# Attention of the diff and moba stages placed between column blocks and output chunks

## The chip, the cores and the metric

The kernel runs on one core of one Trainium2 chip. The metric is the device time of one execution, in microseconds (us). The kernel before took 2924.59 us, the median of 3 runs (2924.18 to 2925.93). All arithmetic is in float32; the large matrix products are made of three products each, of a rounded "high" part and the remaining "low" part of both operands.

## The reference, cut to what matters

The model has 256 tokens of width 1024. Four layers of a first block, each ffn, mixer, ffn, are followed by two layers of a second block. The mixers of the first block are diff, moba, nsa, diff. Those that the change touches:

```
def diff_attention(h, w_in, w_out, lam, subln_g, lambda_init, pos):      # 8 heads
    q, k, v = split(h @ w_in, 3)                    # 1024 x 3072
    q, k = partial_rope(q), partial_rope(k)         # 16 rows of 64: two per head
    lam_full = exp(sum(lam[0] * lam[1])) - exp(sum(lam[2] * lam[3])) + lambda_init
    p = softmax over keys of (q . k) / 8, causal, for both rows c of a head
    a = p[:, :, 0] - lam_full * p[:, :, 1]
    o = a @ v                                       # v: 128 wide per head
    o = rms_norm(o, subln_g, 1e-5) * (1 - lambda_init)
    return o @ w_out

def moba_attention(h, w_in, w_out, pos):                                 # 16 heads
    q, k, v = split(h @ w_in, 3); q, k = partial_rope(q), partial_rope(k)
    # 256 tokens are one block: what is left is causal softmax attention, 64 wide
    return softmax(q . k / 8, causal) @ v @ w_out
```

## The kernel before

**Engines.** Each engine runs its own list of instructions in the order in which the program writes it; semaphores (`s_...`) are the only bond. SyncE (SP) loads the weights, 1 MB a tile, into four buffers RAW in the order of `plan`. Each tile holds two "splits". ScalarE (ACT) writes the high part of a split into HI (L1146 or, where a gain of the norm is folded in, two instructions on L1153), VectorE (DVE) the rest into LO (L1484, L1489). There are six HI and six LO buffers: split n can be made when TensorE (PE) has used split n-6 (`s_used`). `split(upto)` on either engine makes all splits before number `upto` that aren't made yet. `taken(n)` on PE waits for LO of split n.

**A mixer stage** (`st.w0` is its first split). PE projects six column blocks of 512 columns, four splits each: `first_block`, then `later_block` (L676), per split 2 row tiles x 6 matmuls of 128x512. In `first_block` the second row tile waits for its part of XL, which DVE makes in `second_rows` (L1636, `low`, L1525) from the transposes of H. ACT copies a finished block out of PSUM into TM (`copy_out`, L1279). DVE rotates q and k (`rotate`, L1690 to L1694). PE transposes each rotated block (`turns_of_qk`, L833, through `turned_block`), eight 128x128 transposes into PSUM banks 4 and 5, and ACT copies them to QT and KT (`turned_out`, L1288). The blocks come in the order q, q, k, k, v, v, and the attention begins when all six are there.

**The attention** goes by eight pairs i: `scores` (L772, banks 0/1 or 2/3 by turns, with a mask added by four bf16 matmuls), `maxima` on DVE (L1696), `exps` on ACT (L1295, four exponentials with sums), for diff the combination of the two rows on DVE (L1757 to L1768), `probs_turned` on PE (banks 4, 5), `probs` on ACT (L1307), `outputs` on PE (L807, banks 6 and 7 by turns), for diff `sums` of squares on ACT (L1342), roots on POOL (`outputs_roots`, L2071), and `in_place` on DVE (L1745, L1785), which writes M. PE runs scores two pairs ahead and issues eight matmuls of `clock` (L794) that nobody reads. For diff, the factor lambda is made on DVE and ACT after the sixth block (L1732 to L1743) from SGN and LM, which POOL loads at the start of the stage (L2083, L2084) after its loads of the next gains.

**The output projection.** `outputs_flipped` transposes four blocks of M a row tile (first half at pair 7), ACT and DVE make XH and XL of them (`high`, `low`), and `rows_by` (L688) runs eight chunks k of 128 rows of the weights, in two groups of four; each group runs row tile t = 0 over its chunks, then t = 1, six matmuls of 128x512 a chunk, accumulated in banks 4 to 7. The second half is flipped in the hook of chunk (k, t) = (3, 0); (4, 0) is the first to need it. `last_hook` transposes rows for the next stage.

**Steps of the loop on ACT and DVE before.** Both make splits one block ahead: after block n they make all before `w0 + 4n + 9` and then copy or rotate, as in

```
                for n in range(6):
                    if n >= 1:
                        split(st.w0 + 4 * n + 9)
                    copy_out(st, n, TM[:, :, n * 512:(n + 1) * 512], 2 * ((n + 1) % 2), 512)
```

## Time and profile before

| | |
|---|---|
| median of 3 runs | 2924.59 us |
| profiled execution, its own time | 2921.73 us |
| its span | 2919.9 us |
| PE busy | 2847.3 us, 98% |
| weight loads of PE | 2305.9 us, 79% |
| DVE busy | 1857.9 us, 64% |
| ACT busy | 1546.3 us, 53% |
| mean granted clock of PE | 0.996 |

The profile is of one execution. Busy time of an engine is the union of its instructions; matmuls overlap their neighbours, so a short idle stretch of PE can hide in the tail of the last one. The diff stages lie at 205 to 330 and 1782 to 1907 us of the span, moba at 714 to 838 us.

### The profile page before, as it was taken

What the parts mean: (1) busy time and instruction counts of PE and PEld (TensorE: products, weight loads), DVE (VectorE), ACT (ScalarE), POOL (GpSimd) and SP (SyncE); (2) the same over time, 40 slices, a digit from 0 to 9 for tenths busy, and PEclk for the clock granted to TensorE, in tenths of its full rate; (3) what the DMA queues carried; (4) which work ended last, traced back from release to release, by engine and by line L of the source; (5) the groups of instructions that cost most, each with busy time, mean ns of one, the idle gap of its engine ahead of it and who ended that gap; (6) DMA issues with size and microseconds to landing.
All of it is one profiled execution on the core that took longest, in us unless ns stands there. A gap on an engine that the chain in (4) does not pass through costs nothing.

```text
span 2919.9 us, 34940 instructions
## 1 busy us (share of the span) xinstructions
PE 2847.3 (98%) x13484; PEld 2305.9 (79%) x13484; DVE 1857.9 (64%) x2728; ACT 1546.3 (53%) x2656; POOL 149.1 (5%) x254
## 2 busy tenths in 40 slices
PE   8999999999999999999999999899999999999998
PEld 7877787887788788778887878788787788787786
DVE  6766776676567667646676776667654754645654
ACT  6546654654665365446654646665354444444442
POOL 1010100001000000100001000000100000000000
PEclk9999999999999999999999999999999999999999
DMA  8664467566446666551666675366664565654652
GB/s 261 217 222 162 142 213 242 182 225 215 159 152 216 231 191 229 201 162 44 195 222 218 216 250 184 100 216 227 213 229 145 186 202 186 215 193 137 188 187 87
DMA packets 358631, 559.42 MB, mean 192 GB/s; under 512 B 14625, under 2 KB 246049, under 8 KB 358209
## 3 DMA queue, kind: packets, MB, share of 16 engines
q1 hardware_dynamic: 350720, 535.02, 55.7%
q0 software_dynamic: 7600, 21.81, 2.2%
q8 instruction: 107, 1.75, 0.2%
q14 instruction: 60, 0.48, 0.1%
q10 hardware_dynamic: 144, 0.36, 0.0%
HBM read 556.03 MB, written 1.10 MB: 191 GB/s over the span
## 4 chain that ended last, share of the span: by engine, by line
PE 92%; DVE 5%; ACT 1%; issue 1%; POOL 1%; DMA 0%; SPq 0%; DVEq 0%; ACTq 0%; POOLq 0%
PE ps L640 38%; PE ps L701 26%; PE ps L646 19%; PE ps L610 4%; PE ps L813 1%; PE ps L782 1%; PE ps L760 1%; DVE LO L1484 1%; PE ps L928 0%; POOL ST L2021 0%; DVE XL L1525 0%; ACT SB L1303 0%; PE ps L790 0%; DVE M L1563 0%; DVE M L1602 0%
## 5 line engine op out<-in xcount | busy, mean ns | idle before, releaser
L640 PE MATMUL ps<-HI,XH 128*128 128x512 f32 (+1 forms) x2496 | 982.4, 394 | 5.6 <-DVE LO L1489 2.8
L640 PE MATMUL ps<-LO,XH 128*128 128x512 f32 (+1 forms) x2496 | 969.6, 389 | 0.0
L1484 DVE TENSOR_TENSOR LO<-RAW,HI 128x1024 fp32r<-128x1024 f32 x468 | 567.4, 1222 | 368.2 <-ACT HI L1146 366.7
L646 PE MATMUL ps<-HI,XL 128*128 128x512 f32 (+1 forms) x2496 | 769.5, 389 | 0.3
L1146 ACT ACTIVATE HI<-RAW 128x1024 fp32r<-128x1024 f32 x468 | 490.2, 1058 | 488.7 <-PE ps L701 320.2
L1489 DVE SCALAR_TENSOR_TENSOR LO<-RAW,GC,HI 128x512 fp32r<-128x512 f32 (+1 forms) x896 | 622.2, 744 | 188.9 <-ACT HI L1153 186.3
L1153 ACT ACTIVATE HI<-RAW,GC 128x512 fp32r<-128x512 f32 (+1 forms) x896 | 587.9, 714 | 157.8 <-PE ps L646 130.7
L640 PEld LDWEIGHTS ps<-HI,XH 128*128 128x128 f32 x2496 | 469.3, 188 | 102.0 <-DVE LO L1489 4.4
L646 PEld LDWEIGHTS ps<-HI,XL 128*128 128x128 f32 x2496 | 466.6, 188 | 103.4 <-DVE XL L1525 6.8
L640 PEld LDWEIGHTS ps<-LO,XH 128*128 128x128 f32 x2496 | 469.8, 188 | 91.8
L701 PE MATMUL ps<-HI,AH 128*128 128x512 f32 x880 | 281.3, 401 | 0.0
L701 PE MATMUL ps<-LO,AH 128*128 128x512 f32 x880 | 277.6, 397 | 0.0
L701 PE MATMUL ps<-HI,AL 128*128 128x512 f32 x880 | 277.4, 396 | 0.0
L701 PEld LDWEIGHTS ps<-HI,AH 128*128 128x128 f32 x880 | 162.6, 188 | 57.1 <-issue 20.7
L701 PEld LDWEIGHTS ps<-HI,AL 128*128 128x128 f32 x880 | 165.8, 188 | 40.5
L701 PEld LDWEIGHTS ps<-LO,AH 128*128 128x128 f32 x880 | 165.7, 188 | 40.3
L1247 ACT ACTIVATE AH<-ps 128x512 fp32r<-128x512 f32 x110 | 65.8, 598 | 191.2 <-PE ps L610 191.2
L1648 DVE TENSOR_TENSOR AL<-ps,AH 128x512 fp32r<-128x512 f32 x110 | 75.9, 690 | 107.7 <-ACT AH L1247 107.7
L1266 ACT ACTIVATE SG<-ps,ST 128x256 f32<-128x256 f32 x176 | 74.0, 471 | 132.7 <-PE ps L646 132.7
L1662 DVE SCALAR_TENSOR_TENSOR AF<-ps,ST,SG 128x256 f32<-128x256 f32 x176 | 77.0, 479 | 84.7 <-ACT SG L1266 84.7
L1519 DVE SCALAR_TENSOR_TENSOR ACC<-RAW,CS,ACC 128x512 f32<-128x512 f32 x168 | 126.2, 751 | 5.1
L701 PE MATMUL ps<-HI,XH 128*128 128x512 f32 x288 | 91.7, 400 | 10.8 <-DVE LO L1484 4.3
(182 smaller groups left out, 1990.0 us busy)
## 6 DMA issues: line engine op xcount, KB each, us to landing
RAW<-in_ffn_w_in SPq DMA_DIRECT2D x350, 512.0 KB, 4.9
RAW<-in_ffn_w_out SPq DMA_DIRECT2D x88, 1024.0 KB, 5.0
RAW<-in_w_ada SPq DMA_DIRECT2D x48, 1024.0 KB, 5.2
RAW<-in_w_in SPq DMA_DIRECT2D x44, 1024.0 KB, 5.2
RAW<-in_w_ffn_in SPq DMA_DIRECT2D x88, 512.0 KB, 4.8
RAW<-in_diff_w_in SPq DMA_DIRECT2D x24, 1024.0 KB, 5.1
RAW<-in_w_ffn_out SPq DMA_DIRECT2D x22, 1024.0 KB, 4.9
RAW<-in_moba_w_in SPq DMA_DIRECT2D x12, 1024.0 KB, 5.1
```

The source lines that it names most:

```text
L610: i = e.transpose(dst[:, c * P:(c + 1) * P], v, ident)
L640: e.matmul(ps[:, b + t, 0:nw], XH[:, k, t * P:(t + 1) * P], q[s][:, c * nw:(c + 1) * nw], start=(k == 0 and q is HI), stop=False)
L646: i = e.matmul(ps[:, b + t, 0:nw], XL[:, k, t * P:(t + 1) * P], HI[s][:, c * nw:(c + 1) * nw], start=False, stop=(k == 7))
L701: i = e.matmul(ps[:, 4 + 2 * t + nh, :], x(k, t), q[s][:, nh * 512:nh * 512 + 512], start=(k == 0 and q is HI and x is th), stop=(k == chu ...
L1146: e.activation(HI[n % NSPLIT][:, 0:t.width], RAW[t.buf][:, h * t.width:(h + 1) * t.width], ACT.Copy).then_inc(s_hi, 1)
L1153: i = e.activation(HI[n % NSPLIT][:, c * w:(c + 1) * w], RAW[t.buf][:, h * t.width + c * w:h * t.width + (c + 1) * w], ACT.Copy, scale=g[c])
L1266: o = e.activation(SG[:, i, t], ps[:, b + t, 0:S], ACT.Silu, scale=r)
L1484: e.tensor_tensor(LO[n % NSPLIT][:, 0:w], RAW[t.buf][:, at[1] * w:(at[1] + 1) * w], HI[n % NSPLIT][:, 0:w].bitcast(F32), ALU.subtract).the ...
L1489: i = e.scalar_tensor_tensor(out=LO[n % NSPLIT][:, c * w2:(c + 1) * w2], in0=RAW[t.buf][:, at[1] * w + c * w2:at[1] * w + (c + 1) * w2], s ...
L1519: e.scalar_tensor_tensor(out=A, in0=src, scalar=CS[:, kc:kc + 1], in1=A, op0=ALU.mult, op1=ALU.add).then_inc(s_ada, 1)
L1648: e.tensor_tensor(AL[:, 2 * jp:2 * jp + 2, :], ps[:, b, :].rearrange("p (j n) -> p j n", j=2), AH[:, 2 * jp:2 * jp + 2, :].bitcast(F32), A ...
L1662: o = e.scalar_tensor_tensor(out=AF[:, i, t], in0=ps[:, b + t, S:2 * S], scalar=root_of(st, t)[0], in1=SG[:, i, t], op0=ALU.mult, op1=ALU. ...
```

## The change

A stage's work is now placed by a counter `at`. On PE, `at = 4n + k2` is the place ahead of split k2 of block n (4 to 23), 24 the place between the last block and the output chunks, and 25 to 32 the places behind the chunks (k, t) = (0, 0) to (3, 0) and (0, 1) to (3, 1). ACT and DVE loop over the same `at` and write their part of each step there.

The columns are loaded by pairs of heads: blocks 0 and 1 hold q and k of pairs 0 to 3 (256 columns each), block 2 the v of these, and blocks 3 to 5 the same for pairs 4 to 7. A tile of q and k is two DMAs of 512 KB. `QK` takes the place of QT and KT; the rotation has its own room `R` instead of M. PSUM: scores in banks 6 and 7 (the last pair in 2 and 3), turned probabilities in 4 and 5 (the last two pairs in 0 and 1), outputs in bank 5 for pairs 0 to 3 and 0 to 3 for the others. The matmuls of `clock` in these stages are gone. POOL's part is unchanged.

```diff
+PAIR_BLOCKS = ((0, 1024), (256, 1280), (2048,), (512, 1536), (768, 1792), (2560,))
+QK_BLOCKS = (0, 1, 3, 4)
+QK_AT = (6, 10, 18, 22)
+SCORES_AT = (7, 9, 13, 16, 19, 21, 23, 25)
+TURNED_AT = (9, 11, 15, 18, 21, 23, 27, 29)
+OUTPUTS_AT = (13, 14, 16, 19, 25, 26, 28, 30)
+HALF_AT = 22
+SCORE_BANK = (6, 6, 6, 6, 6, 6, 6, 2)
+TURNED_BANK = (4, 4, 4, 4, 4, 4, 0, 0)
+OUTPUT_BANK = (5, 5, 5, 5, 0, 1, 2, 3)
...
@@ block.tensor
                 for k2 in range(4):
+                    if between is not None:
+                        between(4 * n + k2)
                     w = st.w0 + 4 * n + k2
                     taken(w)
...
+                def turned_qk(q):
+                    n = QK_BLOCKS[q]
+                    e.wait_ge(s_rt, c["rt"] + q + 1)
+                    if q == 1:
+                        e.wait_ge(s_pt, c["pt"] + 1)
...
+                def pair_scores(i):
+                    q = i // 2
+                    if i % 2 == 0:
+                        e.wait_ge(s_tn, c["tn"] + 2 * q + 2)
+                    if i == 7:
+                        e.wait_ge(s_ol, c["ol"] + 2)
+                    elif i >= 1:
+                        e.wait_ge(s_ex, c["ex"] + i)
...
+                def pair_turned(i):
+                    e.wait_ge(s_df if diff else s_ex, c["df" if diff else "ex"] + i + 1)
+                    if i < 6:
+                        e.wait_ge(s_tn, c["tn"] + 2 * sum(at <= TURNED_AT[i] for at in QK_AT))
+                        if 1 <= i:
+                            e.wait_ge(s_pt, c["pt"] + i)
+                        placed = sum(at < TURNED_AT[i] for at in OUTPUTS_AT)
+                        if placed:
+                            e.wait_ge(s_o, c["o"] + placed * out)
+                    elif i == 6:
+                        e.wait_ge(s_o, c["o"] + 6 * out)
+                    else:
+                        e.wait_ge(s_pt, c["pt"] + 7)
...
+                def pair_outputs(i):
+                    e.wait_ge(s_cp, c["cp"] + (3 if i < 4 else 6))
+                    e.wait_ge(s_pt, c["pt"] + sum(at < OUTPUTS_AT[i] for at in TURNED_AT))
+                    if 1 <= i < 4:
+                        e.wait_ge(s_o, c["o"] + i * out)
+                        if OUTPUTS_AT[i] > QK_AT[2]:
+                            e.wait_ge(s_tn, c["tn"] + 6)
+                    elif i >= 6:
+                        e.wait_ge(s_ex, c["ex"] + 8)
...
+                def attention(at):
+                    if at in QK_AT:
+                        turned_qk(QK_AT.index(at))
+                    if at in TURNED_AT:
+                        pair_turned(TURNED_AT.index(at))
+                    if at in OUTPUTS_AT:
+                        pair_outputs(OUTPUTS_AT.index(at))
+                    if at in SCORES_AT:
+                        pair_scores(SCORES_AT.index(at))
+                    if at == HALF_AT:
+                        e.wait_ge(s_cp, c["cp"] + 5)
+                        half_flipped(0, 2)
...
-                        later_block(st, n, 512)
+                        later_block(st, n, 512, attention)
...
+                e.wait_ge(s_pt, c["pt"] + 6)
+                e.wait_ge(s_ex, c["ex"] + 7)
+                attention(24)
...
+                def ready(k, t):
+                    if k == 0:
+                        e.wait_ge(s_ol, c["ol"] + t + 1)
+                    elif k == 4:
+                        e.wait_ge(s_ol, c["ol"] + t + 3)
+                def hook(k, t):
+                    if k < 4:
+                        attention(25 + k + 4 * t)
+                    if (k, t) == (3, 1):
+                        half_flipped(1, 0)
+                    last_hook(st, k, t, 8)
...
@@ block.scalar
+                for at in range(33):
+                    if at in (4, 8, 12, 16, 20, 24):
+                        block_out(at // 4 - 1)
+                    if at - 1 in SCORES_AT:
+                        i = SCORES_AT.index(at - 1)
+                        if i == 0 and diff:
+                            lambdas()
+                        exps(st, i, SCORE_BANK[i])
+                    if 4 <= at < 24:
+                        split(st.w0 + at + 6)
+                    if at in QK_AT:
+                        q = QK_AT.index(at)
+                        turned_out(st, q, QK[:, q])
+                    if at in TURNED_AT:
+                        i = TURNED_AT.index(at)
+                        probs(st, i, nj, TURNED_BANK[i])
+                    if at in OUTPUTS_AT and diff:
+                        sums(OUTPUTS_AT.index(at))
+                    if at == HALF_AT:
+                        for t in range(2):
+                            high(t, 0, 2 + t, s_of, c["of"] + t + 1, s_oh)
+                for t in range(2):
+                    high(t, 1, t, s_of, c["of"] + t + 3, s_oh)
+                split(st.w1 + 2)
...
@@ block.vector
+            def by_places(st, softened, placed, placed_after):
+                TM, QK = st.t["TM"], st.t["QK"]
+                second_rows(st)
+                for at in range(33):
+                    if 4 <= at < 24:
+                        split(st.w0 + at + 5)
+                    if at in SCORES_AT:
+                        i = SCORES_AT.index(at)
+                        maxima(st, i, SCORE_BANK[i])
+                    if at % 4 == 0 and at // 4 - 1 in QK_BLOCKS:
+                        n = at // 4 - 1
+                        rotate(st, QK_BLOCKS.index(n), TM[:, :, n * 512:(n + 1) * 512].rearrange("p t (h d) -> p t h d", d=64),
+                               8, cst("c8"), cst("s8"), n, st.t["R"])
+                    if at - placed_after in OUTPUTS_AT:
+                        placed(OUTPUTS_AT.index(at - placed_after))
+                    if at - 1 in SCORES_AT:
+                        softened(SCORES_AT.index(at - 1))
+                    if at == HALF_AT:
+                        for t in range(2):
+                            low(t, 0, 2 + t, s_oh, st.c["oh"] + t + 1, s_ol)
+                for t in range(2):
+                    low(t, 1, t, s_oh, st.c["oh"] + t + 3, s_ol)
+                split(st.w1 + 2)
...
@@ diff on block.vector
+                def lambdas():
+                    e.wait_ge(s_mixw, c["mixw"] + 32)
+                    e.tensor_scalar(SGN[:, :], SGN[:, :], 1.0 - linit, None, ALU.mult).then_inc(s_sgn, 1)
+                    e.tensor_tensor(LM[:, 0:4:2, :], LM[:, 0:4:2, :], LM[:, 1:4:2, :], ALU.mult).then_inc(s_lam, 1)
+                    e.wait_ge(s_lam, c["lam"] + 1)
+                    e.tensor_reduce(LS[:, 0:2], LM[:, 0:4:2, :], AX.X, ALU.add).then_inc(s_lam, 1)
...
+                def softened(i):
+                    if i == 0:
+                        lambda_full()
                     reciprocals(st, i)
...
+                phase(st)
+                lambdas()
+                by_places(st, softened, placed, 1)
...
@@ moba on block.vector
+                by_places(st, softened, placed, 0)
```

`placed` is `in_place` of before. `softened` is the reciprocals and, in diff, the combination.

## Rows read from the trace of the kernel before

**Rows 1.** The page, busy time and share of the span by engine.

```profile
PE 2847.3 (98%) x13484; PEld 2305.9 (79%) x13484; DVE 1857.9 (64%) x2728; ACT 1546.3 (53%) x2656; POOL 149.1 (5%) x254
```

**Rows 2.** Timeline of PE, a diff stage's blocks: start, duration, engine, line, operation, tiles.

```profile
240.22 0.48 PE L640 MATMUL ps<-HI,XH 128*128 128x512 f32 x1
...
251.22 1.03 PE L610 MATMUL ps<-CST,TM 128*128 128x128 f32 x8
```

**Rows 3.** Stretches: width, busy time (and instructions) of each engine, granted clock, DMA.

```profile
275.00:306.00 31.00, 23.63 (x184) 16.63 (x185) 23.70 (x80) 25.53 (x106) 6.00 (x14) 1.00 0.06 19
```

**Rows 4.** Timeline of PE, scores of two pairs in the diff attention.

```profile
287.42 0.93 PE L782 MATMUL ps<-KT,QT 64*128 64x128 f32 x8
...
289.68 0.93 PE L782 MATMUL ps<-KT,QT 64*128 64x128 f32 x8
```

**Rows 5.** Timeline of PE, start of moba's attention; in brackets idle before, and releaser.

```profile
785.56 0.93 PE L782 MATMUL ps<-KT,QT 64*128 64x128 f32 x8 [1.45 <-ACT TM L1279]
...
787.85 2.80 PE L796 MATMUL ps<-CST 128*128 128x384 f32 x8
```

**Rows 6.** Timeline of ACT behind the first column block of a diff stage.

```profile
216.96 1.27 ACT L1279 ACTIVATE TM<-ps,ST 128x512 f32<-128x512 f32 x2 [3.73 <-PE ps L646]
218.12 8.69 ACT L1153 ACTIVATE HI<-RAW,GC 128x512 fp32r<-128x512 f32 x14
```

**Rows 7.** Timeline of DVE: low parts; reciprocals and combination of a pair.

```profile
219.60 9.36 DVE L1489 SCALAR_TENSOR_TENSOR LO<-RAW,GC,HI 128x512 fp32r<-128x512 f32 x14
...
300.70 0.18 DVE L1707 RECIPROCAL RC<-SM 128x4 f32<-128x4 f32 x1
...
301.17 0.75 DVE L1766 SCALAR_TENSOR_TENSOR SB<-SB,CF 128x128 f32<-128x128 f32 x2
```

**Rows 8.** The chain that ended last: exponentials of two pairs.

```profile
278.95 3.33 ACT SB L1303 x16
```

**Rows 9.** Timeline of PE: the first use of XL's second row tile.

```profile
212.23 0.62 PE L646 MATMUL ps<-HI,XL 128*128 128x512 f32 x2
```

**Rows 10.** Timeline of POOL: issue of the load of LM.

```profile
215.91 0.54 POOL L2084 DMA_DIRECT2D LM<-in_diff_lambda  x1
```

**Rows 11.** The tile LM: from issue to landing.

```profile
DMA to landing us min/median/max: 4.6/5.3/6.0
```

**Rows 12.** Timeline of ACT: a table load and its activation, in nsa.

```profile
1287.92 1.28 ACT L1381 ACT_TABLE_LOAD   x1
1289.22 0.28 ACT L1381 ACTIVATE GS<-TM 128x96 f32<-128x96 f32 x1
```

**Rows 13.** Timeline of PE: last outputs of diff, flips of the second half.

```profile
305.36 0.91 PE L813 MATMUL ps<-TM,PT 128*128 128x128 f32 x6 [1.00 <-DVE M L1752]
...
311.58 1.03 PE L610 MATMUL ps<-CST,M 128*128 128x128 f32 x8
```

**Rows 14.** Timeline of DVE: the last placing, low parts of the second half.

```profile
308.39 0.61 DVE L1752 SCALAR_TENSOR_TENSOR M<-ps,ST,SGN 128x128 f32<-128x128 f32 x2
...
312.85 1.29 DVE L1525 TENSOR_TENSOR XL<-ps,XH 128x512 fp32r<-128x512 f32 x2 [2.71 <-ACT XH L1172]
```

**Rows 15.** The page, costliest groups: busy and mean ns, idle before them.

```profile
L1484 DVE TENSOR_TENSOR LO<-RAW,HI 128x1024 fp32r<-128x1024 f32 x468 | 567.4, 1222 | 368.2 <-ACT HI L1146 366.7
```

**Rows 16.** Timeline of PE: the three gaps over 2 us after the start.

```profile
1288.87 14.02 PE L928 MATMUL ps<-RAW,E 128*60 128x256 f32 x64 [2.08 <-DVE E L1827]
...
1372.87 0.73 PE L701 MATMUL ps<-HI,XH 128*128 128x512 f32 x2 [2.17 <-DVE LO L1484]
...
2100.85 1.97 PE L610 MATMUL ps<-CST,M 128*128 128x128 f32 x8 [2.04 <-DVE M L1614]
```

**Rows 17.** Stretches behind these gaps; the column before the last two is the granted clock.

```profile
1290.00:1300.00 10.00, 10.00 (x48) 6.19 (x47) 0.00 (x0) 1.18 (x2) 0.00 (x0) 1.00 0.60 196
...
1374.00:1377.00 3.00, 3.00 (x9) 2.32 (x8) 3.00 (x3) 0.61 (x1) 0.00 (x0) 0.50 0.59 157
...
2104.00:2108.00 4.00, 4.00 (x11) 3.13 (x10) 4.00 (x6) 2.18 (x5) 0.00 (x0) 0.54 0.40 103
```

More of the change, by code:

```diff
@@ L196, in tile_cols, with tiles_pairs, dst @@
                              2 * nw, what, st))
+        def tiles_pairs(w, st):
+            for cols in PAIR_BLOCKS:
+                for half in range(2):
+                    src = w[half * 512:(half + 1) * 512, :].rearrange("(c p) n -> p c n", p=P)
+                    n = 512 // len(cols)
+                    loads = []
+                    for g, c0 in enumerate(cols):
+                        def dst(r, g=g, n=n):
+                            return r[:, :].rearrange("p (c g n) -> p c g n", c=4, n=n)[:, :, g, :]
+                        loads.append((dst, src[:, :, c0:c0 + n]))
+                    plan.append(Tile("w", loads, HW, None, st))
         def tiles_proj(w, st):
@@ L226, in build @@
             else:
-                tiles_proj(a[f"{st.kind}_w_in"][st.j], st)
+                (tiles_proj if st.kind == "nsa" else tiles_pairs)(a[f"{st.kind}_w_in"][st.j], st)
                 if st.kind == "nsa":
@@ L886, in diff_or_moba @@
-            def diff_or_moba(st):
+                out = 2 if diff else 1
+                def turned_qk(q):
[3 more added lines that the diff above has]
+                        e.wait_ge(s_pt, c["pt"] + 1)
+                    elif q == 2:
+                        e.wait_ge(s_pt, c["pt"] + 3)
+                        e.wait_ge(s_o, c["o"] + 3 * out)
+                    elif q == 3:
+                        e.wait_ge(s_pt, c["pt"] + 5)
+                    for t in range(2):
+                        i = turn(ps[:, 4 + t, :], [TM[:, t, n * 512 + j * P:n * 512 + (j + 1) * P] for j in range(4)])
+                    i.then_inc(s_tb, 1)
@@ new lines, in pair_turned @@
+                def pair_turned(i):
[11 more added lines that the diff above has]
+                        e.wait_ge(s_pt, c["pt"] + 7)
+                    for j in range(nj):
+                        o = turn(ps[:, TURNED_BANK[i] + j, :], [SB[:, i % 3, j, m * P:(m + 1) * P] for m in range(3)])
+                    o.then_inc(s_pf, 1)
@@ new lines, in half_flipped @@
+                def half_flipped(half, b):
+                    e.wait_ge(s_o, c["o"] + 4 * (half + 1) * out)
+                    for t in range(2):
+                        flip(t, half, b + t, s_of)
+                def attention(at):
[10 more added lines that the diff above has]
+                        half_flipped(0, 2)
@@ L1327, in diff_or_moba, with block_out @@
                 second_rows(st)
-                for n in range(6):
-                    if n >= 1:
-                        split(st.w0 + 4 * n + 9)
+                def block_out(n):
                     copy_out(st, n, TM[:, :, n * 512:(n + 1) * 512], 2 * ((n + 1) % 2), 512)
-                    if 1 <= n <= 4:
-                        X = QT if n < 3 else KT
-                        turned_out(st, n - 1, X[:, 4 * ((n - 1) % 2):4 * ((n - 1) % 2) + 4, :])
-                for i in range(2):
-                    exps(st, i)
-                if diff:
-                    LS = st.t["LS"]
-                    e.wait_ge(s_lam, c["lam"] + 2)
-                    e.activation(LS[:, 2:4], LS[:, 0:2], ACT.Exp).then_inc(s_lex, 1)
                 def sums(i):
@@ L1674, in ffn, with rotate @@
                 split(st.w1 + 2)
-            def rotate(st, n, v, half, cos, sin):
+            def rotate(st, n, v, half, cos, sin, block=None, free=None):
                 nh = v.shape[2]
                 size = 2 * nh * half
-                R = [M[:, :, :].rearrange("p a b -> p (a b)")[:, j * size:(j + 1) * size]
-                     .rearrange("p (t h d) -> p t h d", t=2, h=nh) for j in range(4)]
+                free = M[:, :, :].rearrange("p a b -> p (a b)") if free is None else free
+                R = [free[:, j * size:(j + 1) * size].rearrange("p (t h d) -> p t h d", t=2, h=nh) for j in range(4)]
                 cb, sb_ = (f.rearrange("p (t d) -> p t d", t=2).unsqueeze(2).to_broadcast([P, 2, nh, half])
@@ L1725, in diff @@
             def diff(st):
                 c, x = st.c, st.t
[L1727 removed]
+                SB, SM, RC, CF, LM, LS, SGN = (x[v] for v in ("SB", "SM", "RC", "CF", "LM", "LS", "SGN"))
                 linit = 0.8 - 0.6 * math.exp(-0.3 * st.i)
[L1729 to L1732 removed]
```

176 lines of the change are left out of this document (58 added, 118 removed).

## Prediction

> **What bounds the kernel now.** I read the page first: TensorE is busy 98% of the span [rows 1], so time moves only by PE work that goes or by PE waits that come or go. The clock is full nearly everywhere. Then the stretches by engine and the timeline of PE: within a diff stage PE runs without a hole through the six column blocks, about 2.75 us for each quarter block of 12 matmuls (11.0 us between the turns of two blocks [rows 2]), until the attention starts. That takes 31.0 us [rows 3], and 0.2 before it in which PE could have gone on. A pair of heads costs PE 2.26 us from one scores to the next where nothing holds it [rows 4], eight pairs 18.1 us, the eight turns of outputs about 0.8: 18.9 us of need. The other 12.3 us are waits and the eight matmuls of `clock`. In moba, whose pairs have twice the turns and outputs, PE is full but for 1.45 us of wait plus 0.2 of pipeline tail, and 2.7 of `clock` [rows 5]: 4.3 us. So all that the change can win is 2 x 12.3 + 4.3 = 28.9 us, 1.0% of the run.
>
> **What it takes away.** Exactly that: `clock` goes, and the chain scores, maxima, exponentials, combination, turn, outputs of each pair is stretched over slots that hold other matmuls. I credit the whole 28.9 us. The PE work itself is the same in number; but each group put between projections costs the first matmul behind it 0.08 to 0.1 us (0.48 instead of 0.39 in [rows 2]), some 15 new places a stage: 1.2 us x 3 = 3.6 us.
>
> **What it adds: waits.** Queues are in order, so I follow each engine's written order through a stage, with slot n meaning `at == n`, and time 0 at the place named. The costs: copy of a block out of PSUM, done 1.4 us after the last matmul; a high part 1.24 (8.69 for seven) [rows 6]; a low part 1.34 (9.36 for seven) [rows 7]; turned copies 1.1, a little under the two copies of the same size in [rows 6]; exponentials of a pair 1.65 (3.33 for two) [rows 8]; reciprocal to combined probabilities 1.2 (300.70 to 301.92 [rows 7]); rotation 1.35 (from the copy's end to the first low part in [rows 6, 7]).
>
> 1. Head of each diff stage. VectorE now runs `lambdas` before `second_rows`, and `lambdas` waits for the two loads of POOL's software queue. The second is issued at 215.91 and lands 4.6 to 6.0 us later, median 5.3 [rows 10, 11]: 221.2. POOL's issue is untouched: it follows the row roots. Three small operations (0.8) and the first low part of XH (0.65) bring 222.7. PE wants that low part for the second row tile at 212.23 [rows 9]. Wait: 10.5 us (9.8 to 11.2 by the landing). Before, this DVE work sat behind the sixth block, and nobody waited for the loads.
> 2. Slot 6, all stages. VectorE now makes three low parts before it rotates block 0. First high part ready at 2.6 after slot 4 starts; low parts until 6.65; rotation until 8.1. Slot 6 starts at 5.5: 2.7 us (before, the rotation came first).
> 3. Slot 9. The exponentials of pair 0 stand behind `block_out(1)` on ScalarE. From the start of slot 8: copy to 1.4, table load and its follower 1.3 (1287.92 to 1289.22 [rows 12]), in diff the small exponential 0.25, exponentials to 4.65, combination to 5.9. PE is at slot 9 after 2.75: 3.15 us in diff; moba waits for the exponentials alone: 1.7.
> 4. Slot 14, diff: one bank (5) for outputs 0 to 3, and the placing of outputs 0 stands behind maxima and a low part: 0.7.
> 5. Slot 18: the transposes of block 3 and the turned probabilities share bank 4, so PE waits for a high part (1.24 + 0.2) and the turned copies (1.1), less the 0.8 of its own turns: 1.8 in all three.
> 6. Slot 21: as 3, behind `block_out(4)`, and on VectorE behind a rotation and a placing: ready at 4.95 against 2.75, 2.2 in diff; 0.35 in moba.
> 7. Before the output rows: PE waits for the exponentials of pair 6, which stand behind `block_out(5)`: 1.4 + 1.65 + 0.1 = 3.15 in all three. This is the old start of the attention, kept, without the maxima.
> 8. Slot 27, diff: turned pair 6 waits for outputs 5 to be placed. From outputs to placed takes 3.6 us (305.36 to 309.0 [rows 13, 14]), and the squares now stand behind the exponentials of pair 7: ready about 9.1 after the rows start, PE there at 6.8: 2.3.
> 9. The second half of the rows: the flip comes directly before the chunk that needs it. From the flip's start the two low parts end after 2.56 (311.58 to 314.14 [rows 13, 14]); behind them VectorE still has to make the weights' low part of that very chunk (`split(st.w0 + at + 5)` ends one short), 1.22 [rows 15]. 3.85 less 0.8 of flips: 3.05 in all three, and 0.3 more in diff for the last placing. Before, the flip had a whole group of chunks ahead of its use.
>
> Sum of diff: 10.5 + 2.7 + 3.15 + 0.7 + 1.8 + 2.2 + 3.15 + 2.3 + 3.35 = 29.85. Sum of moba: 2.7 + 1.7 + 1.8 + 0.35 + 3.15 + 3.05 = 12.75. Two diff stages and moba: 72.45 us of waits, + 3.6 of switches, - 28.9: **+47 us**. Each of the places could be off by 0.5 us; places that are hidden after all would have to give 47 us back.
>
> **The clock.** Waits have a second price. In this trace three gaps of PE passed 2 us in mid-run: after 2.17 us the granted clock was soon 0.50, for 3 us at least; after 2.04 eight transposes took 1.97 us, where they take 1.03 at full clock [rows 2], and the 4 us behind them had 0.54; after 2.08 it stayed at 1.00 [rows 16, 17]. The levels are 1.2 and 2.4 GHz. The first cost at least 1.5 us, the second 0.9 + 1.8. The change makes some 7 gaps over 2 us in a diff stage and 3 in moba, 17 in all; two of three, at 2.1, is 24 us, of which some 4 fall where PE would wait anyway: I take **+20**, between 0 (none falls) and 40 (all fall).
>
> **Other parts.** A block's tile is loaded in two DMAs with 1 KB rows instead of one with 2 KB. The ffn stages load so already, and SP's waits do not change: 0, up to 1 us a stage. The table load is not new, only earlier: one in each stage. The page "ScalarE: Activation LUTs" of the Trainium skill, section What ACT_TABLE_LOAD costs, says that a switch of tables costs 2.66 us with a drain behind the load. The trace does not agree: the load of 1.28 us is followed by its activation 1.30 us after its start [rows 12]. By the page, place 3 would be 1.4 longer in each stage, 4 us in all; I go by the row.
>
> **The number.** The profiled execution took 2921.7 us (span 2919.9). 2921.7 + 47 + 20 = 2988.7; the median of the runs shown is 2.9 higher: 2992.
>
> **Rivals.**
> - The waits as worked out, but the clock holds through gaps of 3 us, as it held through one of 2.08: 2972. For it: the attention of before ran with gaps up to 1.45 us at 1.00. Against it: two of three. 0.15.
> - The waits, and every gap over 2 us lowers the clock, for as long as after 2.04: 3012 to 3020. 0.10.
> - The loads of `lambdas` land early or the head wait costs much less, since PE's first matmuls of the second tile and the clock hide part: two times 10.5 go, with it 4 of clock: 2967. The issue time is in the trace, so 0.06.
> - It does what it says and is faster: VectorE and ScalarE, busy 23.7 and 25.5 of the 31 us [rows 3], get slack from the projections around them, so each chain fits into its two slots. The place is the PE queue, the price 28.9 less 3.6: 2899. It decides the sign once the waits of a diff stage stay under 11 us and of moba under 3. Places 1 and 9 alone are 13.8 in diff, and neither depends on how loaded an engine is, only on the written order. 0.03.
> - Only two fifths of the waits come, 29 us: + 3.6 - 28.9 is +4, 2928, no change that can be told: 0.03.
> - Forecast, 2992, within 15 us: the rest, 0.63.
>
> What a measurement of this kernel can tell from no change is about 0.2%, 5.8 us. Slower by more than that 0.94, within it 0.03, faster 0.03. The range runs from 2957 (the waits 10 us shorter and no clock lost, or no head wait) to 3014 (nearly all gaps at the lower clock).
>
> **What would show it.** In the waits of PE of the changed kernel: a wait of about 10 us on a low part of XH near 212 us and once more near 1800; one near 3 us on the transposes of TM, released by DVE's rotation, three times; waits of about 3 us on the exponentials before the first output chunk and on a low part of weights at the fifth chunk, three times each; no matmul of `clock` but at the start and in nsa. The stretch from the first column matmul of a diff stage to its last output matmul should grow by 17 to 28 us, of moba by 9 to 14. A granted clock under 1.00 should show behind the long gaps. I am wrong if PE passes from the sixth block into the output rows without a hole, or if the first low part of the second row tile is made before the two loads land; a time under 2925 would mean that the engines do not keep the written order as I read it.

## The result

The changed kernel took 2990.9 us (median of 4 runs, 2988.5 to 2991.5) beside 2924.5 for the kernel before in the same comparison (4 runs, 2924.2 to 2925.9). The ratio is 1.0225, 95% interval 1.0207 to 1.0242: 66.4 us slower. 2992 had been forecast.

The page of the changed kernel, busy time by engine (the row that answers to [rows 1]; its span is 2989.0 us, the mean granted clock 0.985 where it was 0.996):

```profile
PE 2867.2 (96%) x13460; PEld 2316.9 (78%) x13460; DVE 1855.3 (62%) x2728; ACT 1543.8 (52%) x2656; POOL 150.1 (5%) x254
```

PE did 24 matmuls fewer (those of `clock`, 8.4 us by [rows 5] three times) and was still busy 19.9 us longer: the matmuls that stayed took 28 us more, the switches between groups included. The other engines did what they had done.

Where PE waited, by the line that waits and the instruction waited for: total, times, longest. Only the lines that are new or have grown:

```profile
PE ps L679 <- DVE XL L1628: 17.1, 2, 8.6
PE ps L736 <- DVE LO L1587: 12.4, 8, 2.7
PE ps L643 <- DVE SB L1886: 10.1, 4, 3.1
...
PE ps L736 <- issue: 9.0, 3, 3.0
PE ps L643 <- DVE TM L1797: 7.7, 3, 2.6
PE ps L643 <- DVE M L1897: 5.6, 4, 2.4
...
PE ps L643 <- issue: 4.9, 4, 1.6
...
PE ps L643 <- ACT SB L1397: 1.9, 2, 1.7
...
PE ps L848 <- DVE M L1897: 1.2, 2, 0.6
```

Names of the changed kernel: L679 and L673 are the column blocks, L736 the output rows, L643 transposes, L817 scores, L848 outputs; on DVE L1628 is `low`, L1797 the end of the rotation, L1886 the combination, L1897 the placing, L1587 and L1592 low parts of weights. Counts of 3 are one in each changed stage, of 2 one in each diff stage. Of the eight waits on L1587, five (4.3 us) stand in the kernel before too; the other three are 8.1.

The same waits in order of time, in the first diff stage. This is the timeline of PE, its rows with idle time before them:

```profile
221.14 1.22 PE L679 MATMUL ps<-HI,XL 128*128 128x512 f32 x2 [8.62 <-DVE XL L1628]
...
235.81 1.97 PE L643 MATMUL ps<-CST,TM 128*128 128x128 f32 x8 [2.57 <-DVE TM L1797]
...
250.87 0.55 PE L643 MATMUL ps<-CST,SB 128*128 128x128 f32 x3 [3.11 <-DVE SB L1886]
...
271.76 0.91 PE L848 MATMUL ps<-TM,PT 128*128 128x128 f32 x6 [0.62 <-DVE M L1897]
...
275.88 0.52 PE L643 MATMUL ps<-CST,SB 128*128 128x128 f32 x3 [0.48 <-DVE M L1897]
...
288.99 0.52 PE L643 MATMUL ps<-CST,SB 128*128 128x128 f32 x3 [1.56 <-issue]
...
301.59 0.55 PE L643 MATMUL ps<-CST,SB 128*128 128x128 f32 x3 [1.94 <-DVE SB L1886]
...
318.00 1.19 PE L736 MATMUL ps<-HI,XH 128*128 128x512 f32 x2 [3.01 <-issue]
...
330.10 0.52 PE L643 MATMUL ps<-CST,SB 128*128 128x128 f32 x3 [2.35 <-DVE M L1897]
...
344.63 1.22 PE L736 MATMUL ps<-HI,XH 128*128 128x512 f32 x2 [2.71 <-DVE LO L1587]
```

Read the durations too. Two matmuls of 128x512 in a row took 0.62 us before [rows 9], and 1.22 here at 221.14. Eight transposes of TM took 1.03 [rows 2], and 1.97 here at 235.81. Those ran at half clock. The stretches say the same (width, busy time of PE, PEld, DVE, ACT and POOL, granted clock, DMA share, GB/s; the first beside [rows 9] and [rows 10], where PE had no hole):

```profile
205.00:225.00 20.00, 11.38 (x46) 8.83 (x45) 8.74 (x17) 7.64 (x20) 5.41 (x9) 0.75 0.31 96
...
248.00:262.00 14.00, 11.13 (x56) 8.91 (x57) 7.74 (x19) 9.55 (x28) 0.00 (x0) 0.88 0.31 87
262.00:275.00 13.00, 12.38 (x67) 9.92 (x66) 8.46 (x19) 8.73 (x26) 2.12 (x4) 1.00 0.43 150
...
318.00:330.00 12.00, 9.75 (x42) 7.43 (x42) 4.85 (x17) 3.22 (x16) 1.81 (x4) 0.75 0.01 1
```

From the first matmul of the diff stage to the first of the next stage it was 124.9 us before (204.76 to 329.69) and is 153.2 (204.89 to 358.08): 28.3 longer. In moba 123.9 (713.92 to 837.81) became 138.3 (742.30 to 880.60): 14.4 longer. The second diff stage went from 124.9 (1782.42 to 1907.34) to 150.9 (1825.18 to 1976.04), 25.9 longer. The three are 68.6 us, of the 69.1 by which the span grew.

How much of this is clock can be added up: PE's busy time in stretches of 1 us, times what the granted clock lacks of 1.00. Over the three stages that gives 25.2 us here (11.4, 4.8 and 9.0), and 0.0 in the kernel before. Below it is called the clock sum.

### The profile page after: what moved, and what is told of

Read it like the earlier page. It is cut to its first block, busy times and chain, and to the rows that moved or that the text cites. A ratio compares the mean times of both kernels' runs of the same rounds, so it can differ in the third digit from the quotient of the medians.

```text
span 2989.0 us, 34946 instructions
## 1 busy us (share of the span) xinstructions
PE 2867.2 (96%) x13460; PEld 2316.9 (78%) x13460; DVE 1855.3 (62%) x2728; ACT 1543.8 (52%) x2656; POOL 150.1 (5%) x254
## 4 chain that ended last, share of the span: by engine, by line
PE 89%; DVE 6%; ACT 2%; issue 2%; POOL 1%; DMA 1%; SPq 0%; DVEq 0%; ACTq 0%; POOLq 0%
PE ps L673 36%; PE ps L736 26%; PE ps L679 18%; PE ps L643 4%; PE ps L848 2%; PE ps L817 1%; DVE LO L1592 1%; PE ps L795 1%; DVE LO L1587 1%; DVE XL L1628 1%; POOL ST L2136 1%; ACT JUNK L1259 0%; PE ps L1021 0%; PE ps L825 0%; ACT TM L1372 0%
## 5 line engine op out<-in xcount | busy, mean ns | idle before, releaser
L673 PE MATMUL ps<-HI,XH 128*128 128x512 f32 (+1 forms) x2496 | 989.5, 397 | 5.6 <-DVE LO L1592 2.3
L673 PE MATMUL ps<-LO,XH 128*128 128x512 f32 (+1 forms) x2496 | 972.9, 390 | 0.0
L679 PE MATMUL ps<-HI,XL 128*128 128x512 f32 (+1 forms) x2496 | 772.8, 391 | 17.3 <-DVE XL L1628 17.1
L1587 DVE TENSOR_TENSOR LO<-RAW,HI 128x1024 fp32r<-128x1024 f32 x468 | 566.3, 1222 | 341.9 <-ACT HI L1239 340.6
L1592 DVE SCALAR_TENSOR_TENSOR LO<-RAW,GC,HI 128x512 fp32r<-128x512 f32 (+1 forms) x896 | 622.3, 744 | 205.3 <-ACT HI L1246 204.2
L679 PEld LDWEIGHTS ps<-HI,XL 128*128 128x128 f32 x2496 | 468.4, 189 | 122.4 <-DVE XL L1628 24.7
L673 PEld LDWEIGHTS ps<-HI,XH 128*128 128x128 f32 x2496 | 471.9, 189 | 102.5 <-DVE LO L1592 4.3
L673 PEld LDWEIGHTS ps<-LO,XH 128*128 128x128 f32 x2496 | 472.2, 189 | 91.6
L736 PE MATMUL ps<-HI,AH 128*128 128x512 f32 x880 | 281.3, 401 | 0.0
L736 PE MATMUL ps<-LO,AH 128*128 128x512 f32 x880 | 277.6, 397 | 0.0
L736 PE MATMUL ps<-HI,AL 128*128 128x512 f32 x880 | 277.4, 396 | 0.0
L736 PEld LDWEIGHTS ps<-HI,AH 128*128 128x128 f32 x880 | 162.6, 188 | 57.1 <-issue 20.7
L736 PEld LDWEIGHTS ps<-HI,AL 128*128 128x128 f32 x880 | 165.8, 188 | 40.5
L736 PEld LDWEIGHTS ps<-LO,AH 128*128 128x128 f32 x880 | 165.7, 188 | 40.3
L736 PE MATMUL ps<-HI,XH 128*128 128x512 f32 x288 | 97.4, 420 | 27.8 <-DVE LO L1587 12.4
```

What stands on the lines that cost most here:

```text
L673: e.matmul(ps[:, b + t, 0:nw], XH[:, k, t * P:(t + 1) * P], q[s][:, c * nw:(c + 1) * nw], start=(k == 0 and q is HI), stop=False)
L679: i = e.matmul(ps[:, b + t, 0:nw], XL[:, k, t * P:(t + 1) * P], HI[s][:, c * nw:(c + 1) * nw], start=False, stop=(k == 7))
L736: i = e.matmul(ps[:, 4 + 2 * t + nh, :], x(k, t), q[s][:, nh * 512:nh * 512 + 512], start=(k == 0 and q is HI and x is th), stop=(k == chu ...
L1587: e.tensor_tensor(LO[n % NSPLIT][:, 0:w], RAW[t.buf][:, at[1] * w:(at[1] + 1) * w], HI[n % NSPLIT][:, 0:w].bitcast(F32), ALU.subtract).the ...
L1592: i = e.scalar_tensor_tensor(out=LO[n % NSPLIT][:, c * w2:(c + 1) * w2], in0=RAW[t.buf][:, at[1] * w + c * w2:at[1] * w + (c + 1) * w2], s ...
```

## The experiments

The theory under test: the loss is a handful of waits that come from the order in which DVE and ACT are written, plus the clock that the gaps cost. If so, orders alone must undo it, with the places, banks and loads left as they are. The rivals: the waits are only where PE happens to stand, so that one removed comes back at the next place; or the waits matter and the clock does not.

**`lambdas` later.** The changed kernel, with DVE's part of `lambdas` moved from ahead of `second_rows` to place 6:

```diff
-                lambdas()
-                by_places(st, softened, placed, 1)
+                by_places(st, softened, placed, 1, lambdas)
@@ in by_places, behind the split of each place
+                    if at == 6 and early is not None:
+                        early()
```

> The changed kernel with one step moved back: in a diff stage VectorE does the operations on SGN and LM at place 6, behind the low parts of the second row tile, and no longer ahead of them. My theory (the order written on each engine makes the waits): the two waits of PE on XL, 8.6 and 8.4 us, go, and with them the stretch at the lower clock behind them, some 2 us each: 22 us less than the 2991 of the changed kernel, about 2969. Rival 1 (only the wait counts, not the clock): 17 less, 2974. Rival 2 (the loads of SGN and LM are late for whoever wants them, so the wait only moves to place 6 or 9): nothing regained, 2985 to 2991.

Measured: 2973.1 us (2970.3 to 2974.9), ratio 1.0162 [1.0147, 1.0177], 17.8 us under the changed kernel. Both waits on XL of 8.6 us are gone, and 205 to 225 us is at clock 1.00. But 17.8 is hardly more than the two waits, 17.1: the time is rival 1's. It is not that the clock costs nothing: the clock sum is 25.6 us, where it was 25.2. What the head no longer costs is lost elsewhere. Stretches of 4 us show one such place. First the changed kernel behind its head gap (first row) and behind the gap at slot 9, then this kernel behind its gap at slot 9:

```profile
221.00:225.00 4.00, 3.86 (x9) 3.12 (x10) 2.00 (x4) 0.00 (x0) 0.00 (x0) 0.50 0.16 37
...
250.00:254.00 4.00, 3.13 (x19) 2.35 (x20) 3.33 (x9) 2.28 (x5) 0.00 (x0) 0.80 0.20 24
254.00:258.00 4.00, 4.00 (x20) 3.30 (x19) 2.42 (x6) 2.67 (x10) 0.00 (x0) 0.78 0.63 239
```

```profile
239.00:243.00 4.00, 2.89 (x16) 1.91 (x16) 2.31 (x6) 2.54 (x5) 0.00 (x0) 0.59 0.11 13
243.00:247.00 4.00, 4.00 (x13) 3.14 (x12) 3.24 (x9) 1.72 (x8) 0.00 (x0) 0.55 0.67 249
```

The same gap of 3.11 us cost more clock here (0.59 and 0.55) than there (0.80 and 0.78). The head gap cost 8.6 us of wait and 2.3 of slower matmuls: from slot 6's transposes back to the stage's start the stretch is 10.96 us shorter (235.81 less 224.85). From these transposes to the outputs at slot 14 it is 37.5 us here (224.85 to 262.34) and was 35.95 (235.81 to 271.76): 1.5 of the 2.3 came back. Whether this is because the head gap no longer stands ahead of it isn't shown. The gap of 2.6 at slot 6 stands 12 us ahead of it in both kernels, and in the second diff stage of the changed kernel, behind a head gap of 8.4 and the same gap at slot 6, the gap of 3.11 left the clock at 1.00:

```profile
1871.78 0.55 PE L643 MATMUL ps<-CST,SB 128*128 128x128 f32 x3 [3.11 <-DVE SB L1886]
```

```profile
1872.00:1876.00 4.00, 4.00 (x27) 3.04 (x26) 3.46 (x7) 2.38 (x10) 0.00 (x0) 1.00 0.44 110
```

So one gap at one place has no fixed price in clock; a number can be given for the sum only.

**The gaps filled.** The changed kernel, with matmuls that nobody reads in front of the long waits:

```diff
@@ tokens_by, ahead of the matmuls with XL
+                if beside is not None:
+                    beside()
@@ first_block
+                              (lambda: clock(12)) if st.kind == "diff" and k2 == 0 else None).then_inc(s_used, 1)
@@ turned_qk
+                    if q == 0:
+                        clock(3)
                     e.wait_ge(s_rt, c["rt"] + q + 1)
@@ pair_turned
+                    if i == 0:
+                        clock(4 if diff else 2, 5)
                     e.wait_ge(s_df if diff else s_ex, c["df" if diff else "ex"] + i + 1)
@@ ahead of the output rows
                 e.wait_ge(s_pt, c["pt"] + 6)
+                clock(4, 4)
                 e.wait_ge(s_ex, c["ex"] + 7)
@@ hook of the chunk (3, 1)
                         half_flipped(1, 0)
+                        clock(3, 2)
```

> The changed kernel with matmuls that nobody reads put ahead of five waits of PE, each group a little shorter than the gap that it fills: 24 at the head of a diff stage (8.2 of 8.6 us), 6 at place 6, 8 at place 9 (4 in moba), 8 ahead of the output rows, 6 ahead of chunk (4, 0). The waits end when they did; only the idleness goes. My theory (a gap lowers the granted clock and that is a price of its own, forecast at 20 us): the clock stays near 1.00 in these stages and the time falls by 15 to 25, to about 2971. Rival (the clock falls but PE would have waited anyway, or the lower clock costs nothing here): 2988 to 2993, and if the groups are too long, more.

Measured: 2974.4 us (2973.5 to 2975.3), ratio 1.0167 [1.0152, 1.0182]: 16.6 us less, with all the waits' causes in place. The mean clock rose from 0.985 to 0.993, and the first stretch (PE's 19.07 us include the filling) to 1.00:

```profile
205.00:225.00 20.00, 19.07 (x78) 13.45 (x77) 8.58 (x17) 7.57 (x20) 5.41 (x9) 1.00 0.33 100
```

The clock sum fell from 25.2 to 3.4. So the clock cost at least 16.6 us; the filling doesn't reach every gap and can itself delay work.

**Exponentials first.** The changed kernel, with ACT's copy of a block behind the exponentials at slots 8, 20 and 24:

```diff
-                    if at in (4, 8, 12, 16, 20, 24):
+                    if at in (4, 12, 16):
                         block_out(at // 4 - 1)
...
                         exps(st, i, SCORE_BANK[i])
+                    if at in (8, 20, 24):
+                        block_out(at // 4 - 1)
```

> The changed kernel with one order changed on ScalarE: at places 8, 20 and 24 the exponentials come ahead of the copy of the finished block. My theory: the wait before the output rows (3.0 us in three stages) goes whole; at place 9 moba's 1.7 goes and diff keeps about 1.5 of 3.1, since VectorE still rotates block 1, which needs the copy, ahead of the combination; place 21 stays in diff for the same reason. Waits regained: 3 x 3.0 + 2 x 1.6 + 2.0 = 14, with the clock behind the gap at the rows some 5 more: about 2972. Rival (the copy comes later by as much, and the rotation, the turns and outputs 4 wait for it): 2985 to 2991.

Measured: 2974.6 us (2973.9 to 2977.4), ratio 1.0170 [1.0154, 1.0185], 16.4 less. The three waits of 3.0 before the output rows fell to 1.1 in all, moba's on the exponentials are gone, and that on the combination at slot 9 is 2.1 instead of 3.1, with the table load still in the chain; 11.7 of the 16.4 are these waits:

```profile
PE ps L643 <- DVE SB L1888: 8.2, 4, 2.1
...
PE ps L736 <- issue: 1.1, 3, 0.4
```

**The head alone, in the kernel before.** The kernel before, with DVE's operations on SGN and LM ahead of `second_rows`, and nothing else:

```diff
-                second_rows(st)
-                for n in range(6):
-                    projected(st, n, TM, n * 512, 512 if n < 4 else 0)
+                phase(st)
                 e.wait_ge(s_mixw, c["mixw"] + 32)
                 e.tensor_scalar(SGN[:, :], SGN[:, :], 1.0 - linit, None, ALU.mult).then_inc(s_sgn, 1)
-                for i in range(2):
-                    maxima(st, i)
                 e.tensor_tensor(LM[:, 0:4:2, :], LM[:, 0:4:2, :], LM[:, 1:4:2, :], ALU.mult).then_inc(s_lam, 1)
...
                 e.tensor_reduce(LS[:, 0:2], LM[:, 0:4:2, :], AX.X, ALU.add).then_inc(s_lam, 1)
+                second_rows(st)
+                for n in range(6):
+                    projected(st, n, TM, n * 512, 512 if n < 4 else 0)
+                for i in range(2):
+                    maxima(st, i)
```

> The kernel before with one part of the change alone: VectorE does the operations on SGN and LM at the head of a diff stage, ahead of the low parts of the second row tile. My theory: PE waits about 8.5 us in each of the two diff stages and runs some us at the lower clock behind it: +21, 2945. Rival 1 (no price of the clock): +17, 2941. Rival 2 (the wait comes from something else that the change brings, as the loads in halves): 2924 to 2928.

Measured: 2948.1 us (2946.5 to 2950.6), ratio 1.0079 [1.0062, 1.0096]: 22.9 us for two waits of 8.7, so 5.6 beyond them. The clock sum is 7.9, of it 4.8 behind the head; the rest lies in the attention, where PE also waits. The order of three small operations accounts for a third of what the change lost, without any of the change's own work.

```profile
PE ps L646 <- DVE XL L1525: 17.3, 2, 8.7
```

**Rotation and low part.** The changed kernel, with block 0 rotated ahead of the low part of place 4, and the low part that the chunk (4, 0) needs made at place 24:

```diff
-                    if 4 <= at < 24:
+                    if 4 < at < 24:
                         split(st.w0 + at + 5)
...
+                    if at == 24:
+                        split(st.w0 + 29)
```

> The changed kernel with two orders changed on VectorE: at place 4 it rotates block 0 ahead of the three low parts, and at place 24 it also makes the low part of the fifth chunk's weights. My theory: the wait at place 6 (2.6 us) goes in three stages, the one ahead of chunk (4, 0) shrinks by 1.2, together 11.4, and some 4 us of lower clock behind them: about 2976. Rival 1 (no price of the clock): 2979.5. Rival 2 (the low parts are then late for PE at places 5 to 7): 2985 to 2991.

Measured: 2978.4 us (2968.2 to 2981.2), ratio 1.0175 [1.0160, 1.0190], 12.5 less. Slot 6 no longer waits (7.7 us gone), and the wait on the late low part went down by 7.4; but `low` of XL now ends last before (4, 0), 1.1 each time, 3.3 more in all: of 3.05 forecast for that place a third is the flip itself. The waits account for 11.8 of the 12.5, so hardly any clock came back; at 2978.4 the time lies nearer to rival 1 (2979.5) than to 2976.

```profile
PE ps L736 <- DVE XL L1628: 7.3, 7, 1.1
...
PE ps L736 <- DVE LO L1587: 5.0, 8, 2.2
```

**All orders together.** The three order changes above, ACT's copy of the turned block ahead of the high part at slot 18, and DVE's combination ahead of its rotation and placing:

```diff
+                    if at == 18:
+                        turned_out(st, 2, QK[:, 2])
                     if 4 <= at < 24:
                         split(st.w0 + at + 6)
...
                         maxima(st, i, SCORE_BANK[i])
+                    if at - 1 in SCORES_AT:
+                        softened(SCORES_AT.index(at - 1))
                     if at % 4 == 0 and at // 4 - 1 in QK_BLOCKS:
...
                         placed(OUTPUTS_AT.index(at - placed_after))
-                    if at - 1 in SCORES_AT:
-                        softened(SCORES_AT.index(at - 1))
```

> The changed kernel with all these orders changed at once: operations on SGN and LM at place 6, rotation of block 0 first, exponentials ahead of the block copy at 8, 20 and 24, the combination ahead of rotation and placing, turned copies of block 3 ahead of the high part, low part of the fifth chunk's weights at place 24. Waits that should go, from the changed kernel's trace: diff 8.5 + 2.6 + 3.1 + 1.9 + 3.0 + 1.2 + 1.2 = 21.5, twice; moba 2.6 + 1.7 + 0.1 + 3.0 + 1.2 + 1.2 = 9.8; 53 in all, and most of the lower clock, 17: about 2921, between 2915 and 2932. So my theory says that the placing itself is sound and about even with the kernel before, and that the written order cost all the rest. Rival (new waits take the place of these, engines being behind): 2940 or more.

Measured: 2928.8 us (11 runs, 2927.6 to 2933.2), ratio 1.0016 [1.0007, 1.0025]. Orders alone gave back 62 of the 66 us; the 2921 expected was missed by 8. Slot 18 gave back 0.35 of its 1.2. What was left had in part been made by the last edit: with the combination ahead, the placing came late, and the one bank of outputs 0 to 3 held PE at slot 14 for 2.3 us instead of 0.6, and slot 27 as before for 2.4:

```profile
PE ps L643 <- DVE M L1905: 7.9, 8, 2.4
...
PE ps L848 <- DVE M L1905: 4.6, 2, 2.3
```

**The kernel before without `clock`.** One line less, the eight matmuls of each diff and moba stage:

```diff
                     scores(st, i, row(QT, i), row(KT, i))
-                clock()
```

> The kernel before without the eight matmuls of clock in the diff and moba stages. My theory: they lie where PE would wait for exponentials anyway, so at most 0.7 us a stage comes back, 2923 to 2925, if the clock holds; if it falls in the gap of 2 us or more that they leave, some 2 us a stage more: up to 2932. Rival (they cost their whole 2.7 us in each of three stages): 2916.

Measured: 2928.8 us (10 runs, 2924.3 to 2931.4), ratio 1.0012 [1.0003, 1.0021]. That is 3.7 us more than the 2925.1 beside it. The matmuls are worth what they take and a little more: their 2.7 us a stage became waits for exponentials and combination, and behind these the clock fell:

```profile
280.84 0.97 PE L782 MATMUL ps<-KT,QT 64*128 64x128 f32 x8 [1.88 <-ACT SB L1302]
...
284.14 0.90 PE L610 MATMUL ps<-CST,SB 128*128 128x128 f32 x3 [1.79 <-DVE SB L1765]
```

```profile
280.00:290.00 10.00, 7.37 (x50) 5.30 (x51) 6.44 (x24) 6.56 (x30) 0.00 (x0) 0.66 0.00 1
```

**The loads in two DMAs.** The kernel before, with each tile of the diff and moba columns as two DMAs of 512 KB with 1 KB rows:

```diff
+                for half in range(2):
...
+                    for g in range(2):
+                        loads.append((dst, src[:, :, c0 + 256 * g:c0 + 256 * g + 256]))
```

> The kernel before with one part of the change alone: each tile of the diff and moba column blocks in two DMAs of 512 KB with rows of 1 KB, columns in the old order. My theory: nothing waits for these loads, 2923 to 2926. Rival (the loads in halves are late or slow): 2928 or more.

Measured: 2924.2 us (10 runs, 2921.5 to 2925.6), ratio 0.9996 [0.9987, 1.0005]: no cost that can be told.

**The orders mended.** From the waits that were left in the kernel with all orders: the combination goes ahead of placing and rotation only at slots 8 and 20, the turned block's copy goes ahead of the high part at slot 6 too, and the turned pair 6 goes to bank 2, where it needs no placing. ACT and DVE also make the split of the sixth chunk's weights (`split(st.w0 + 30)`) at places 30 and 31 instead of at the end. The parts that aren't orders of ACT or DVE, and DVE's places 8 and 20:

```diff
-TURNED_BANK = (4, 4, 4, 4, 4, 4, 0, 0)
+TURNED_BANK = (4, 4, 4, 4, 4, 4, 2, 0)
...
                     elif i == 6:
-                        e.wait_ge(s_o, c["o"] + 6 * out)
+                        e.wait_ge(s_ex, c["ex"] + 8)
                     else:
                         e.wait_ge(s_pt, c["pt"] + 7)
+                        e.wait_ge(s_o, c["o"] + 6 * out)
...
+                    if at in (8, 20):
+                        softened(SCORES_AT.index(at - 1))
+                        if at - placed_after in OUTPUTS_AT:
+                            placed(OUTPUTS_AT.index(at - placed_after))
```

> The pairs version with all order changes of e6_all_orders, and what its remaining waits point to: the combination goes ahead of the placing and rotation only at slots 8 and 20; the copies of the turned pair stand before the high part at slots 6 and 18; the turned pair 6 goes to another bank. In e6_all_orders each diff stage still held TensorE at slots 7 (0.61 us), 14 (2.31), 21 (1.02) and 27 (2.40) on VectorE's placing. Theory (what is left of the loss is these in-order waits): each diff stage loses 1.7 less at slot 14, 2.4 less at slot 27, 0.9 less at slot 21 and 0.6 less at slot 7, 5.6 us in all, each moba stage 0.9, so 2928.7 - 13 = 2915.7, and a few us of clock with it: 2912 to 2917, faster than before. Rival (VectorE is nearly full in these stretches, so that a wait removed at one slot comes back at the next): at or above 2925, with new waits of TensorE on VectorE's low parts or flips of the same sum.

Measured: 2910.9 us (5 runs, 2908.2 to 2912.9) beside 2925.8, ratio 0.9950 [0.9936, 0.9963]: 14.9 us faster than the kernel before, and 80 faster than the change as it was made. Its busy time, and all waits of PE in the first diff stage (205 to 330 us):

```profile
PE 2841.4 (98%) x13460; PEld 2300.6 (79%) x13460; DVE 1855.5 (64%) x2728; ACT 1543.2 (53%) x2656; POOL 150.1 (5%) x254
```

```profile
PE ps L643 <- issue: 1.2, 1, 1.2
PE ps L736 <- DVE XL L1634: 1.1, 1, 1.1
PE ps L848 <- DVE M L1913: 0.6, 1, 0.6
PE ps L643 <- DVE M L1913: 0.5, 1, 0.5
PE ps L736 <- issue: 0.4, 1, 0.4
```

3.8 us where the changed kernel has 27, with the same work on every engine and the same places. So waits taken away did not come back elsewhere. The clock sum is 0.0 again.

## Why the prediction was right, step by step

**The sign** was right, and by the reason given: all nine places are in the trace. Seven have the named releaser; the trace puts slot 18 and the wait before the output rows down to PE's own issue. The second fell from 3.0 to 0.4 with ACT's exponentials ahead of its copy, so the experiment names it. At slot 18 PE goes on at 288.99, 0.1 us after ACT's two copies of the turned block end (287.83 to 288.89 on its timeline). With these copies ahead of the high part the wait fell only from 1.6 to 1.2: most of it is the copies themselves, which can't start before PE's own transposes end. The place was right; what it owed to the high part is 0.35.

**The sizes of the waits**, forecast and found in us: head 10.5, 8.6; slot 6 2.7, 2.6; slot 9 3.15, 3.1 (moba 1.7, 1.7); slot 14 0.7, 0.6; slot 18 1.8, 1.6; slot 21 2.2, 1.9 (moba 0.35, 0.25); before the rows 3.15, 3.0; slot 27 2.3, 2.35; chunk (4, 0) 3.35 in diff and 3.05 in moba, 2.7 in both. One of 0.5, at the second placing, was not forecast. A diff stage has 27.0 instead of 29.85, moba 11.8 instead of 12.75: 65.5 in all where the sum had 72.45. For slot 18 and chunk (4, 0) the sum took PE's own eight turns as 0.8 us, though [rows 13] have 1.03; slot 18's turns took 1.03 and chunk (4, 0)'s 1.09, and both waits came out shorter for it. The switches were priced against a matmul of 0.39, which stands in none of the rows shown; PE's timeline before has one at 204.76 us.

Most of what is missing is the head. Its term took the landing of LM from the kernel before, 5.3 us after the issue [rows 11]. In the changed kernel it landed in 3.5:

```profile
DMA to landing us min/median/max: 3.4/3.5/3.6
```

So the size of the head wait did not follow from the written order alone, as the prediction had it. The wait seems to shorten its own cause: while PE stands, SP's weight loads stop, and the DMA engines are busy 0.31 of 205 to 225 us instead of 0.50. In the five kernels whose head waits the median is 3.4 to 3.6, and 4.8 to 5.3 in the six whose head doesn't. With the gaps filled, where PE is busy (19.07 of 20 us) and the DMA share stays at 0.33, it is 3.5 as well, so it isn't the idle PE that matters; that the emptier DMA engines do is what is left, and was not tested by itself.

**The place of the table load** was right, and with it the row's price instead of the page's. In the timeline of ACT at slot 8:

```profile
245.08 1.27 ACT L1372 ACTIVATE TM<-ps,ST 128x512 f32<-128x512 f32 x2 [2.60 <-PE ps L679]
246.36 1.28 ACT L1438 ACT_TABLE_LOAD   x1
247.66 0.20 ACT L1438 ACTIVATE LS<-LS 128x2 f32<-128x2 f32 x1
```

The load follows the copy by 0.01 us and is followed by its activation after 1.30. The page "ScalarE: Activation LUTs" of the Trainium skill, section What ACT_TABLE_LOAD costs, adds a drain of 1.38 us to a load of 1.28. This trace agrees with the load and shows no drain behind it; with one, as an estimate by that page, slot 9 would have waited 4.5 us and not 3.1.

**What was credited and the switches.** The mended kernel tests both: its waits are 3.8 + 3.8 + 2.7 = 10.3 us, so 10.3 + 3.6 of switches - 28.9 gives -15.0 against the kernel before, and -14.9 was measured. The two terms were right together, to the 4 us of the interval; nothing here tests them one by one. That `clock` taken out alone costs 3.7 us is no contradiction: what it covered is now covered by projections.

**The clock** was the term with the wrong size. 66.4 - 65.5 - 3.6 + 28.9 leaves 26 us for it, where 20 was taken, within the bounds of 0 to 40. The clock sum, read from the trace by itself, is 25.2, and the filling gave 16.6 back. (Between the two profiled executions the three stages grew by 68.6, which would leave 28; some 3 us of that are not placed.) The working was 17 gaps, two of three falling, 2.1 us each, less 4 us that would be hidden. In the changed kernel 13 of the 17 (1.94 us and longer) had a granted clock under 1.00 in the 4 us behind them; the four others are slot 6 in moba, slot 21 in the first diff stage, and slots 9 and 27 in the second. 25.2 over 13 is 1.9 each, as an average. So the price of a gap was about right, more of them fell, and the 4 us off have nothing in the trace to stand on. The form was rough as well: the model had a gap over 2 us as the condition, but without `clock` the granted clock fell behind gaps of 1.8 and 1.9 us, and it held behind one of 3.11. That the total came out near is luck in part, owed to two errors of opposite sign, waits 7 too long and clock 6 too short. The same sum made for the kernel with `lambdas` later, 65.5 - 17.1 + 3.6 - 28.9, is 23; 47.9 was measured: 25 of clock, though the two longest gaps had gone, and its clock sum is 25.6.

**The rivals.** That the clock holds (2972) is out by the stretches at 0.50 to 0.88. That the head costs little is out by the timeline. That it is faster (2899) was rightly given little, and with the point from which it decides: waits under 11 us in a diff stage and 3 in moba. The mended kernel has 3.8 and 2.7 and is faster; the kernel with all orders, whose waits in the same view come to 9.8 and 3.9, 23.5 in all, would be 2 us faster by the sum and is some 4 slower. Of these 6 us its clock sum explains 1.7: behind the wait of 2.40 at slot 27 the clock was 0.75 over 306 to 309 us and 0.68 over 309 to 312, while it stayed at 1.00 behind the same wait in the second diff stage and behind the waits of 2.31 at slot 14. The stages that the change doesn't touch lost another 3.4 us more than in the kernel before (9.9 and 6.5, added up in the same way), and the rest is open. So this run doesn't decide that point.

**What would show it.** Growth of 17 to 28 us was given for a diff stage and 9 to 14 for moba; it was 28.3 and 14.4, the clock's part being larger.

## What to carry to other kernels

When work of one engine is spread between that of another, the helpers' written orders decide the sign: walk each in-order queue through every place, ask what stands ahead of the one instruction that is waited for, and put copies, low parts and loads that nobody needs yet behind it. A wait on a load at the head of a stage was the longest of them here (8.6 of 27 us), since everything on that engine stands behind it. When the first measurement disappoints, price the waits before giving the placement up: here orders alone were worth 62 us, and with one bank moved as well 80, which turned a loss of 2.3% into a gain of 0.5%.

## What the runs showed of the hardware that was not expected

A small load on POOL's software queue landed 3.3 to 3.8 us after its issue where PE's wait had held up the weight loads (DMA share 0.31 over 205 to 225 us), and 4.6 to 6.0 us where they went on (0.50). The granted clock fell behind gaps of PE of 1.88 and 1.79 us, to 0.66 over 280 to 290 us in the kernel before without `clock`, where the gap of 1.45 at the start of the attention had left it at 1.00 [rows 3, 5]. And one gap at one place, in one and the same execution, can cost clock or not: behind 3.11 us at slot 9 the changed kernel had 0.80 and 0.78 in the first diff stage and 1.00 in the second. With `lambdas` later the first diff stage had 0.59 and 0.55 there. Why is open.
